# Hybrid short-conv / SSD / PEER step: the decay tables behind the first convolution, squares, sample outputs and sample-chunk waits reordered

## The reference

```
h    = rmsnorm(x)
proj = h @ w_in            -> conv mixer B, C, x | SSD z, xBC, dt | gates g_a, g_b
y_a  = (B * conv3(C * x_a)) @ w_a_out
xBC  = silu(conv4(xBC) + bias);  dt = softplus(dt_raw + bias)
cum  = cumsum(dt * a) inside each chunk;  decay_end = exp(cum_last - cum)
y_b  = rmsnorm((chunked SSD scan + D * x) * silu(z)) @ w_ssd_out
x    = x + (sigmoid(g_a) * y_a + sigmoid(g_b) * y_b) @ w_o
x    = x + PEER(rmsnorm(x)): top 16 of 128 x 128 experts by product keys, 8 heads
y    = rmsnorm(x), without the 16 meta tokens
```

## Time and profile before

| what | value |
|---|---|
| runs | 2489.29, 2476.82, 2484.91 us; median 2484.91 |
| profiled execution: time | 2485.15 us |
| its span, first to last instruction | 2482.5 us |
| mean granted TensorE clock | 0.987 of full |
| busy TensorE / its weight loads | 2418.7 us (97%) / 2240.2 us (90%) |
| busy VectorE | 1631.0 us (66%) |
| busy ScalarE | 819.3 us (33%) |
| busy GpSimd | 1423.1 us (57%) |
| DMA | 510.10 MB, 205 GB/s on average |
| chain that ended last | 90% TensorE, 6% VectorE, 2% DMA |

### The profile page before, as it was taken

The page is one execution under the profiler, slowest core; times in us unless marked ns, Lnnn a source line. Parts: engine busy times, 40 slices in busy tenths (PEclk is TensorE's granted clock), DMA queues, the critical chain, the costliest instruction groups (busy, mean ns, idle before and its releaser), DMA issues.

```text
span 2482.5 us, 38027 instructions
## 1 busy us (share of the span) xinstructions
PE 2418.7 (97%) x14472; PEld 2240.2 (90%) x14472; DVE 1631.0 (66%) x2612; ACT 819.3 (33%) x1239; POOL 1423.1 (57%) x787
## 2 busy tenths in 40 slices
PE   9899999999999999999999999999999999999997
PEld 9899999996789999999999999898888999999996
DVE  6765444446786245098997788876596666766663
ACT  4332113231131012233343456565432333333322
POOL 5454333342343555447676667666676777777762
PEclk9999999999999999999999999999999999999998
DMA  5224222226652232247676769888988888888871
GB/s 211 68 77 142 94 86 89 93 100 211 227 190 79 85 124 95 85 138 268 233 260 234 248 212 303 277 281 280 320 310 294 306 310 318 319 315 310 312 246 68
DMA packets 207067, 510.10 MB, mean 205 GB/s; under 512 B 15184, under 2 KB 103632, under 8 KB 204496
## 3 DMA queue, kind: packets, MB, share of 16 engines
q1 hardware_dynamic: 57312, 207.39, 25.5%
q10 hardware_dynamic: 112752, 166.56, 19.0%
q0 software_dynamic: 36864, 134.23, 14.7%
HBM read 424.68 MB, written 83.44 MB: 205 GB/s over the span
## 4 chain that ended last, share of the span: by engine, by line
PE 90%; DVE 6%; DMA 2%; ACT 1%; issue 1%; ACTq 0%; DVEq 0%; SPq 0%
PE ps L856 48%; PE ps L605 29%; PE ps L904 4%; PE ps L750 1%; DVE abuf L1903 1%; PE ps L869 1%; PE ps L630 1%; PE ps L785 1%; DMA x<-xT 1%; PE ps L762 1%; PE ps L758 1%; PE ps L765 1%; PE ps L738 1%; ACTq L1255 0%; PE ps L743 0%
## 5 line engine op out<-in xcount | busy, mean ns | idle before, releaser
L554 POOL TENSOR_SCALAR w_hi<-raw 128x1024 fp32r<-128x1024 f32 x129 | 141.8, 1099 | 565.1 <-issue 430.3
L581 POOL TENSOR_TENSOR w_lo<-raw,w_hi 128x1024 fp32r<-128x1024 f32 x128 | 324.7, 2537 | 211.5 <-PE ps L856 211.3
L581 POOL TENSOR_TENSOR w_lo<-raw,e_hi 128x1024 fp32r<-128x1024 f32 x128 | 323.2, 2525 | 195.1 <-PE ps L856 188.2
L856 PE MATMUL ps<-p_hi,w_lo 128*128 128x448 f32 x1024 | 377.2, 368 | 0.0
L856 PE MATMUL ps<-g_hi,w_lo 128*128 128x448 f32 x1024 | 376.6, 368 | 0.0
L556 POOL TENSOR_TENSOR w_lo<-raw,w_hi 128x1024 fp32r<-128x1024 f32 x129 | 316.9, 2457 | 10.8
L605 PE MATMUL ps<-h_hi,w_hi 128*128 128x296 f32 (+1 forms) x1216 | 277.2, 309 | 8.7 <-ACT line_s L1045 7.6
L605 PE MATMUL ps<-h_lo,w_hi 128*128 128x296 f32 (+1 forms) x1216 | 264.1, 299 | 0.0
L605 PE MATMUL ps<-h_hi,w_lo 128*128 128x296 f32 (+1 forms) x1216 | 263.3, 298 | 0.0
L1230 ACT ACTIVATE e_hi<-raw 128x1024 fp32r<-128x1024 f32 x128 | 135.9, 1061 | 298.9 <-DMA raw<-units 117.4
L605 PEld LDWEIGHTS ps<-h_hi,w_hi 128*128 128x128 f32 x1216 | 197.6, 190 | 30.9 <-issue 21.5
(11 more groups left out here) (326 smaller groups left out, 5365.3 us busy)
## 6 DMA issues: line engine op xcount, KB each, us to landing
raw<-units SPq DMA_DIRECT2D x385, 512.0 KB, 3.7
gate_scratch<-gt ACTq DMA_DIRECT2D x14, 2048.0 KB, 12.9
gbuf<-gate_scratch ACTq DMA_DIRECT2D x32, 896.0 KB, 9.0
activation_scratch<-ge ACTq DMA_DIRECT2D x120, 224.0 KB, 3.8
abuf<-activation_scratch ACTq DMA_DIRECT2D x30, 896.0 KB, 6.0
prev<-ssm_in ACTq DMA_DIRECT2D x8, 1024.0 KB, 6.1
ssm_s<-prev ACTq DMA_DIRECT2D x8, 1024.0 KB, 6.0
parked_tiles<-stage ACTq DMA_DIRECT2D x24, 296.0 KB, 2.1
```

The source lines that it names most:

```text
L554: pool.tensor_scalar(w_hi[:, s, :], raw[:, r, :], 1.0, 1.0, ALU.mult, ALU.mult).then_inc(s_whi, 1)
L581: pool.tensor_tensor(w_lo[:, n % 2, :], raw[:, n % RAW, :], e_hi[m % HS_].bitcast(F32), ALU.subtract)\
L856: last = mm(accp[par], w[:, k * P:(k + 1) * P], x_[:, k, t0:t0 + ND], start=k == 0 and i == 0, stop=k == KT - 1 and i == 2)
```

## The change

What it does, place by place:

- VectorE: `scale_stage(3)`, the wait for the exponentials and everything behind it go into a function `decay_tables()`, called at the start of iteration 1 of the convolution loop, with `scale_stage(3)` last; the memset of `cm` goes to iteration 3. The subtractions and the chunk ends are written to PSUM banks 4 and 5 (`to_end`, `ends`) instead of `sp[2]`, `sp[3]` and `sp[0]`, and the exponential of the subtractions is made in place there, in two pieces.
- ScalarE: the four identity copies, behind `deviation(0)`; the exponentials in iteration 0 of its loop instead of iteration 1; `scaled_out(3)` in iteration 2.
- TensorE, chunks: the wait for `s_state` moves behind `s_bd` and `s_y2`; in the sample chunk's groups 1 to 3 the two head-row matmuls wait for the third state addition only, and `s_state` is waited for behind them.
- Squares: VectorE adds seven of eight; TensorE accumulates eight products on their sum and eight on the last square itself.
- Last group: its eight units are written out instead of looped; the transposes of `osb` stand behind the second unit, and VectorE's addition of them ahead of the third tile.
- End: 14 products of 448 columns into bank 4 between the last squares' sum and the spreading of the roots.

```
@@ constants
+KEEP = 14
+        T_END = CHUNKS[-2][0]
+        ends = ps[0:HEADS, 4, T_END:T_END + NE]
+        def to_end(t0, n):
+            b = int(t0 >= T_END)
+            return ps[0:HEADS, 4 + b, t0 - b * T_END:t0 - b * T_END + n]
@@ TensorE, added_squares
-                pe.wait_ge(s_sqa, KT * (r - GROUPS))
+                a = (KT - 2) * (r - GROUPS)
+                pe.wait_ge(s_sqa, a)
                 for i in range(NT):
-                    last = mm(turned[0:nq, i:i + 1], sqa[:, i * nq:(i + 1) * nq], ones[:, 0:1], start=True, stop=True)
+                    mm(turned[0:nq, i:i + 1], sqa[:, i * nq:(i + 1) * nq], ones[:, 0:1], start=i == 0, stop=False)
+                pe.wait_ge(s_sq, XT + KT * (r - GROUPS))
+                for i in range(NT):
+                    last = mm(turned[0:nq, i:i + 1], squares_of(XT + KT - 1)[:, i * nq:(i + 1) * nq], ones[:, 0:1],
+                              start=False, stop=i == NT - 1)
@@ TensorE, chunks
-                    if s:
-                        pe.wait_ge(s_state, s)
-                    else:
-                        pe.wait_ge(s_dTs, NC + 1)
                     if ys < 0:
+                        if s:
+                            pe.wait_ge(s_state, s)
+                        else:
+                            pe.wait_ge(s_dTs, NC + 1)
...
                     if ys:
                         pe.wait_ge(s_y2, ys)
+                    if sample and g:
+                        pe.wait_ge(s_snew, 4 * g - 1)
+                    else:
+                        pe.wait_ge(s_state, s)
                     for hh in range(2):
...
+                    if sample and g:
+                        pe.wait_ge(s_state, s)
@@ TensorE, last group and end
-            pe.wait_ge(s_osb, 1)
-            for k in range(KT):
-                last = pe.transpose(turned_rows[:, k], osb[:, k * P:(k + 1) * P], ident[:])
-            last.then_inc(s_ot, 1)
-            outputs(NG - 1, 1)
+            pe.wait_ge(s_p, NG * GI)
+            for u in range(KT):
+                m = NKEYS + (NG - 1) * KT + u
+                expert_unit(m, m % HS_, (L0 + m) // 2, (p_hi[1], p_lo[1]), 0)
+                if u == 1:
+                    pe.wait_ge(s_osb, 1)
+                    for k in range(KT):
+                        last = pe.transpose(turned_rows[:, k], osb[:, k * P:(k + 1) * P], ident[:])
+                    last.then_inc(s_ot, 1)
             added_squares(2 + GROUPS)
+            for i in range(KEEP):
+                mm(ps[:, 4, 0:ND], ones_r[:], p_hi[1][:, 0, :], start=True, stop=True)
             spread_out(2 + GROUPS)
@@ ScalarE
+            act.wait_ge(s_c, 1)
+            for i in range(2):
+                a, b = slice(i * HEADS, (i + 1) * HEADS), slice(i * TS, (i + 1) * TS)
+                act.activation(fold[a, :], ident[a, a], ACT.Copy)
+                act.activation(fold2[b, :], ident[b, b], ACT.Copy)
...
-            scaled_out(3)
...
-                if j == 1:
+                if j == 0:
                     act.wait_ge(s_sp, 1)
                     act.activation(dq[64:96, :], dq[0:32, :], ACT.Exp).then_inc(s_de, 1)
-                    act.activation(sp[3][:], sp[2][:], ACT.Exp).then_inc(s_de, 1)
+                    first, rest = to_end(0, T_END), to_end(T_END, T - T_END)
+                    act.activation(first, first, ACT.Exp)
+                    act.activation(rest, rest, ACT.Exp).then_inc(s_de, 1)
+                if j == 2:
+                    scaled_out(3)
@@ VectorE
-            scale_stage(3)
...
-            dve.tensor_copy(fold[0:HEADS, :], ident[0:HEADS, 0:HEADS])
-            dve.tensor_copy(fold[HEADS:, :], ident[HEADS:2 * HEADS, HEADS:2 * HEADS])
-            dve.tensor_copy(fold2[0:TS, :], ident[0:TS, 0:TS])
-            dve.tensor_copy(fold2[TS:, :], ident[TS:2 * TS, TS:2 * TS])
             for c, (t0, n) in enumerate(CHUNKS[:-1]):
-                ts_(sp[2][:, t0:t0 + n], dq[0:32, t0:t0 + n], last_c, -1.0, ALU.subtract, ALU.mult)
+                ts_(to_end(t0, n), dq[0:32, t0:t0 + n], last_c, -1.0, ALU.subtract, ALU.mult)
...
+            def decay_tables():
+                dve.wait_ge(s_de, 2)
...
+                    tt_(dq[96:128, t0:t0 + n], to_end(t0, n), sp[1][:, t0:t0 + n], ALU.mult)
...
+                dve.sem_inc(s_ds, 1)
+                scale_stage(3)
             for j in range(CT):
+                if j == 1:
+                    decay_tables()
+                elif j == 3:
+                    dve.memset(cm[:], 0.0)
...
-            dve.wait_ge(s_ot, 1)
-            xk = x[:, :, T - NS:]
-            tt_(xk, xk, turned_rows, ALU.add).then_inc(s_xs, 1)
             for u in range(KT):
+                if u == 2:
+                    dve.wait_ge(s_ot, 1)
+                    xk = x[:, :, T - NS:]
+                    tt_(xk, xk, turned_rows, ALU.add).then_inc(s_xs, 1)
+                if u > 3:
+                    add_squares(2 + GROUPS, u - 3)
+                if u == KT - 1:
+                    add_squares(2 + GROUPS, u - 2)
+                    add_squares(2 + GROUPS, u - 1)
                 add_tile(NG - 1, u)
-                if u >= 2:
-                    add_squares(2 + GROUPS, u - 1)
-            add_squares(2 + GROUPS, KT - 1)
```

More of the change, by code:

```diff
@@ L235, in trunk @@
         dend = scr("dend", [P, HEADS, NE])
-        sp = [at(f"sp{i}", spos[0] + i * TW, [HEADS, T]) for i in range(4)]
+        sp = [at(f"sp{i}", spos[0] + i * TW, [HEADS, T]) for i in range(2)]
         rows = [at(f"rows{i}", R1 + i * 4 * D, [P, D]) for i in range(XR - 1)]
@@ L956, in square @@
                 a = i - XT
-                if a >= 2:
-                    act.wait_ge(s_sqa, a - 1)
+                if a >= 0 and a % KT >= 2:
+                    act.wait_ge(s_sqa, a // KT * (KT - 2) + max(a % KT - 2, 1))
                 elif a < 0 and i >= 4:
@@ L1526, in _ @@
             cs = sample_view(dq[0:32, TP:T])
-            tt_(sample_view(sp[2][:, TP:T]), cs[:, :, DEC_L - 1:DEC_L].to_broadcast([HEADS, DEC_B, DEC_L]), cs,
+            tt_(sample_view(to_end(TP, TS)), cs[:, :, DEC_L - 1:DEC_L].to_broadcast([HEADS, DEC_B, DEC_L]), cs,
                 ALU.subtract).then_inc(s_sp, 1)
[L1529 to L1533, removed]
@@ L1534, in _ @@
-            dve.tensor_copy(sp[0][:, 1:NC - 1], dq[64:96, N_META + P - 1:TP:P])
-            link(dve.tensor_copy(sp[0][:, NC - 1:NE].rearrange("p (q a b) -> p q a b", q=2, a=2),
-                                 dq[64:96, TP + DEC_L - 1:T:DEC_L].rearrange("p (a q b) -> p q a b", a=2, q=2)))
-            link(tt_(bde[:], ident[0:HEADS, 0:HEADS].unsqueeze(2).to_broadcast([HEADS, HEADS, NE]),
-                     sp[0][:, 0:NE].unsqueeze(1).to_broadcast([HEADS, HEADS, NE]), ALU.mult))
-            link(dve.tensor_copy(cum2[0:HEADS, :], dq[0:HEADS, :]))
@@ L1540, in _ @@
-            tt_(cum2[HEADS:, :], dq[0:HEADS, :], cum2[0:HEADS, :].bitcast(F32), ALU.subtract)
-            link(dve.memset(cm[:], 0.0))
-            dve.sem_inc(s_ds, 1)
+            def decay_tables():
+                dve.wait_ge(s_de, 2)
+                link(dve.tensor_copy(sp[1][:], dq[32:64, :]))
+                for t0, n in ((0, T_END), (T_END, T - T_END)):
+                    tt_(dq[96:128, t0:t0 + n], to_end(t0, n), sp[1][:, t0:t0 + n], ALU.mult)
+                dve.tensor_copy(ends[:, 0:1], dq[64:96, N_META - 1:N_META])
+                dve.tensor_copy(ends[:, 1:NC - 1], dq[64:96, N_META + P - 1:TP:P])
+                link(dve.tensor_copy(ends[:, NC - 1:NE].rearrange("p (q a b) -> p q a b", q=2, a=2),
+                                     dq[64:96, TP + DEC_L - 1:T:DEC_L].rearrange("p (a q b) -> p q a b", a=2, q=2)))
+                link(tt_(bde[:], ident[0:HEADS, 0:HEADS].unsqueeze(2).to_broadcast([HEADS, HEADS, NE]),
+                         ends.unsqueeze(1).to_broadcast([HEADS, HEADS, NE]), ALU.mult))
+                link(dve.tensor_copy(cum2[0:HEADS, :], dq[0:HEADS, :]))
+                link(tt_(cum2[HEADS:, :], dq[0:HEADS, :], cum2[0:HEADS, :].bitcast(F32), ALU.subtract))
+                dve.sem_inc(s_ds, 1)
+                scale_stage(3)
@@ L1721, in add_squares @@
             def add_squares(r, k):
-                a = KT * (r - GROUPS - 1) + k
-                dve.wait_ge(s_sq, XT + a + 1)
+                dve.wait_ge(s_sq, XT + KT * (r - GROUPS - 1) + k + 1)
                 if k == 1:
-                    tt_(sqa[:, 0:TK], squares_of(XT), squares_of(XT + 1), ALU.add).then_inc(s_sqa, 2)
+                    tt_(sqa[:, 0:TK], squares_of(XT), squares_of(XT + 1), ALU.add).then_inc(s_sqa, 1)
                 else:
-                    dve.wait_ge(s_sqa, a)
+                    dve.wait_ge(s_sqa, (KT - 2) * (r - GROUPS - 1) + k - 1)
                     tt_(sqa[:, 0:TK], sqa[:, 0:TK], squares_of(XT + k), ALU.add).then_inc(s_sqa, 1)
@@ L1742, in _ @@
             unscaled_lo(KT, "ffn", KT - 1, gu_hi, gu_lo)
-            add_squares(1 + GROUPS, KT - 1)
             rsqrt(1 + GROUPS, 1.0 / D, 0)
```

## The result

The changed kernel took 2463.53 us (median of 14 runs, 2453.67 to 2473.05) against 2484.47 for the kernel before beside it (14 runs, 2472.83 to 2491.22): a ratio of 0.9925, 95% interval 0.991 to 0.9941, so 20.9 us less. The profiled execution of the changed kernel took 2463.61 us.

The account below looks back on a forecast made before the run. TensorE, busy 97% of the span, was taken as the bound, so only its standstills and low clock could yield time. Terms of 8.7, 4.3, 3.2, 2.2 and 0.2 us sum to 18.6: 2485.15 to 2466.6 us, range 2457 to 2477.

Parts of the forecast that it names:

- Part A: Start of the kernel: first convolution ahead of the decay tables removes TensorE's line-copy stall and slow tile; 8.7 us.
- Part B: Sample chunk: head-row matmuls fill part of three state waits, and two falls of the clock go; 4.3 us.
- rival 2: Sample gaps and kernel end: the clock falls anyway, also under the fillers; 2473.4 us in all, chance 0.13.
- Part C: Last group: TensorE no longer waits for the copied sample outputs, transposes stand behind the second unit; 3.2 us.
- Part D: Added squares: TensorE no longer waits for the last addition, fillers hold the clock; 2.2 us at the end.
- The middle: Middle squares: TensorE's wait of 1.4 us gives way to 1.2 us of matmuls; 0.2 us.
- The sum: Whole kernel: 8.7 + 4.3 + 3.2 + 2.2 + 0.2 = 18.6 us, all on TensorE's path.
- 1 (the stall forms again): Three tiles on: first table copy 5.1 us late and the clock falls; 2472.7 us in all, chance 0.13.
- 3 (VectorE falls behind for good): Settled convolutions: all three passes meet GpSimd's split, TensorE waits in each tile; 2497.5 us, chance 0.03.
- 4 (no change): Start of the kernel: convolution 0 ends too late to release the line; 2485 us, chance 0.03.

Follow-up runs that it names:

- e5: Changed kernel with the decay tables' operands in SBUF tiles instead of PSUM, order kept; 2464.69 us, one run.
- e6: Changed kernel without the 14 filler matmuls at the end; 2462.99 us, one run.
- e9: Changed kernel once more, without an edit, for a second profile; 2460.38 us (4 runs), ratio 0.9908 to the kernel before.
- e10: e4 with 11 filler matmuls at the end instead of 14; 2454.57 us (4 runs), ratio 0.9886 to the kernel before.
- e11: Kernel before with 21 warming matmuls instead of 20; 2487.99 us, one run.
- e4: Changed kernel with six matmuls of the following unit put ahead of each sample-state wait; 2459.38 us (6 runs), ratio 0.9903.

## Why the prediction was right, point by point

- **Part A** was sized at 8.7 us and is 9.5, by mechanism as forecast. The chain that I worked out stands in the profile almost piece by piece: convolution 0 at 59.2 (measured 59.40) to 65.1 (64.9), convolution 1 from 71.3 (71.41), convolution 3 to 85.5 (85.3), the table's copy at 86.7 (86.5). The wait left was 0.6 us instead of 1.4, since TensorE came to it 0.6 us later than I had it and the copy was done 0.2 us earlier. The line copy of channel 3 was in time; that I had it 0.2 us late was a slip, for 71.3 + 2.75 + 1.8 puts the end of convolution 1 at 75.9, not at 77.1 (measured 74.9). The price of 1.7 us for the six subtractions had no row behind it; they took 1.4 us. The estimate from the Trainium skill (VectorE: DVE Perf Modes, "Why PSUM operands drop a tier") was 0.3 us more for the subtractions with PSUM as an operand. The trace agrees for PSUM as the operand written: 1.24 us against 1.00 into SBUF (e5). Even so PSUM was worth 0.8 us in all.
- **Part B** was sized at 4.3 us and brought -0.5 in the first profile. The step that failed is "with 0.9 us of idle left in place of 1.4 I expect no fall": 1.0 us was left, and in the first profile all three gaps had the fall. Counted over all profiles: with the old wait 14 of 15 gaps had a fall (all but the one that I read in the earlier trace rows), with B 5 of 12 (changed 3, e6 2, e5 and e9 none), with the gap filled 0 of 15. The gaps of one execution are not independent, so those 12 are four executions with 3, 2, 0 and 0 falls. On average the three gaps take 33.2 us with the old wait (five profiles) and 29.7 with B (four): 3.5 us, of which about 1.2 us come from B's earlier matmuls in every profile, and 2.3 rest on how often the clock fell in so few executions. I had read one lucky gap as if it were a third of all cases, and so took for a property of the kernel what was one execution's. That part of rival 2 (the gaps keep their low clock) came true in the first profile.
- **Part C** was sized at 3.2 us and is 3.9, in every kernel that has it. I charged 1.3 us for the transposes from their row of before; in the chain they take 0.87. The other 0.3 us are not assigned.
- **Part D** at the end was sized at 2.2 us and was 2.4 in the first profile, but that was the better of its two outcomes, so in part luck: the mean over seven profiles is 7.4 us for the stretch against 9.0 with the old end, 1.6. Rival 2's fall under the fillers happened in four of seven, at 4.51 us instead of my 5.8, since the clock came back before they were through. The middle brought 0.6 instead of 0.2.
- **The sum** of the parts over all profiles is 9.5 + 3.5 + 0.6 + 3.9 + 1.6 = 19.1 us, beside my 18.6; the slower query units take 2.3 of it back, which I had not foreseen, and leave 16.8. The medians say 20.9 us (interval 15 to 22) and, beside e10, 24.1 us (15 to 31). What the medians have over the parts, 4 us or more, is not assigned. The gates' stretch is of that size: against the first profile the three of the kernel before and e11 average -3.2 us there and the other eleven -7.0. But the three alone spread over 11 us, so whether the change moves it, or only the executions differ, stays open. That my total came out is in part luck: errors cancelled, A and C too low against B too high, and places that I had not looked at added about as much as they took.
- **Rivals.** 1 (the stall forms again) did not occur: the wait for the first table copy was 0.6 us, not 5.1. Nor did 3 (VectorE falls behind for good): from convolution 6 on, one pass in three meets the split, as before. 4 (no change) is out.

## What to carry to other kernels

When an in-order engine holds a resource's release behind work that is wanted much later, moving the release ahead can be costed from the trace (here to 0.8 us of 9.5), if each of the next waits on the same engine is followed until one is in time again. A short idle of TensorE should be priced with its clock, and from more than one execution; better still, it is filled with a slice of work that is due anyway: six matmuls ahead of each wait took the gaps from 29.7 us on average to 25.3, in all five profiles that had them (7.1 us less than the changed kernel's first profile, 2.4 less than its second). Fillers without a use need their own comparison: here no gain from them is shown.

The version to keep is one with the filled gaps: e4, or e10, which differs from it in the number of fillers alone. e10 took 0.9886 of the kernel before. Its median is 5.8 us under the changed kernel's on the same chip, but with four runs each their intervals overlap, so that it beats the changed kernel is shown for the gaps by the profiles and not by the times.

## What I had not expected of the hardware

- An idle of 1.0 us in TensorE was followed by a fall of its clock to 1.2 GHz in 5 of 12 cases and one of 1.4 us in 14 of 15; two profiles of one kernel had three falls and none. With the gap filled there was none in 15.
- VectorE's scan over two SBUF operands took 3.46 us where it met GpSimd's split, against 1.4 alone, and a copy of three columns 2.24, against 0.17 alone.
- Of one kernel's two profiles, the stretch of the gates differed by 10.3 us (kernel before) and 2.5 us (changed kernel). Against the first profile the three of the kernel before and e11 stand at 0, -10.3 and +0.7 us there, the other eleven between -2.1 and -9.4. It is the largest single piece of scatter that these profiles show, and it goes with the time that two DMA issues hold ScalarE (12.2 to 21.6 us together).
- The same query units run at 6.24 or 6.40 us, by matmuls 0.130 us apart or with one of every four 0.140 apart; in the fourteen profiles the pace is one or the other throughout the stretch, and what chooses is open.
